# Second block: the values of all heads computed as [token, column] with the normed rows stationary

## The reference, cut to what matters

```python
h = rmsnorm(x, ln_attn_pre)
proj = h @ w_in                  # 1024 -> 3*512 (diff) + 3*512 (fox) + 8
dq, dk = first 512, next 512 columns     # 8 half heads of 64
dv = next 512 columns                    # 4 heads of 128
fq, fk, fv = the next 3 * 512 columns    # 8 heads of 64
f_logit = last 8 columns + b_f; cum = cumsum(log_sigmoid(f_logit))
# per block of 128 query rows, causal:
pd = softmax(dq dk^T / 8 + relative bias);  ad = pd[:, 0] - lam * pd[:, 1]
od = rmsnorm(ad @ dv, subln_g) * (1 - lambda_init)
pf = softmax(fq fk^T / 8 + cum_q - cum_k);  of = pf @ fv
x = x + rmsnorm(concat(od, of) @ w_out, ln_attn_post)
x = x + rmsnorm(square(relu(rmsnorm(x, ln_mlp_pre) @ w_up)) @ w_down, ln_mlp_post)
```

## Time and profile before

| | |
|---|---|
| time, median of 3 (range) | 1090.02 us (1089.85 to 1090.96) |
| the profiled execution | 1090.4 us, span 1089.1 us |
| TensorE busy | 1077.0 us, 99% of the span |
| TensorE weight loads | 885.4 us, 81% |
| ScalarE busy | 562.1 us, 52% |
| VectorE busy | 540.7 us, 50% |
| GpSimd busy | 434.8 us, 40% |
| mean granted TensorE clock | 0.998 |

### The profile page before, as it was taken

One profiled execution on the slowest core, in us unless ns is written; L12 is line 12 of the kernel. 1 busy time (PEld: TensorE's weight loads), 2 busy tenths in 40 slices (PEclk: granted clock), 3 DMA queues, 4 the chain that ended last, 5 costly groups with the idle time before them and its releaser, 6 DMA issues.

```text
span 1089.1 us, 14787 instructions
## 1 busy us (share of the span) xinstructions
PE 1077.0 (99%) x5656; PEld 885.4 (81%) x5656; DVE 540.7 (50%) x1136; ACT 562.1 (52%) x1042; POOL 434.8 (40%) x233
## 2 busy tenths in 40 slices
PE   8999999999999999999999999999999999999998
PEld 7877878787887888898778777789888888888886
DVE  3739799797765234152446455435111115544444
ACT  6546767767777642353556566554222224333333
POOL 4244242352532444552232332345444446444441
PEclk9999999999999999999999999999999999999999
DMA  9134131221312332722223221232333334323212
GB/s 255 52 92 122 40 79 49 69 78 39 97 50 68 90 92 92 249 78 62 79 78 84 72 79 58 85 90 79 97 97 97 97 97 135 99 97 98 95 57 78
DMA packets 140992, 98.02 MB, mean 90 GB/s; under 512 B 9077, under 2 KB 125170, under 8 KB 140922
## 3 DMA queue, kind: packets, MB, share of 16 engines
q1 hardware_dynamic: 139192, 95.83, 30.0%
q10 hardware_dynamic: 1730, 1.25, 0.4%
HBM read 94.93 MB, written 2.91 MB: 90 GB/s over the span
## 4 chain that ended last, share of the span: by engine, by line
PE 86%; DVE 9%; issue 2%; ACT 2%; DMA 1%; SPq 0%; POOL 0%; DVEq 0%; ACTq 0%
PE bank L496 26%; PE bank L1213 14%; PE bank L1231 14%; PE bank L537 5%; PE bank L910 4%; PE bank L884 4%; PE bank L894 4%; PE bank L1244 2%; DVE g L1915 1%; DVE bank L2033 1%; PE bank L511 1%; DVE multipliers L2031 1%; DVE s L2111 1%; PE bank L1059 1%; PE bank L1041 1%
## 5 line engine op out<-in xcount | busy, mean ns | idle before, releaser
L2497 POOL TENSOR_TENSOR ring<-raw_ring,ring 128x1024 fp32r<-128x1024 f32 x160 | 390.0, 2441 | 566.8 <-ACT ring L1258 566.7
L496 PE MATMUL bank<-hT,ring 128*128 128x512 f32 x1536 | 389.9, 401 | 0.5 <-ACT rawsb L1333 0.5
L496 PEld LDWEIGHTS bank<-hT,ring 128*128 128x128 f32 x1536 | 278.4, 188 | 57.1 <-issue 4.9
L1258 ACT CAST ring<-raw_ring 128x1024 fp32r<-128x1024 f32 x160 | 167.2, 1047 | 109.7 <-PE bank L1231 88.9
L1213 PE MATMUL bank<-hT,ring 128*128 128x512 f32 x672 | 152.5, 389 | 0.0
L1231 PE MATMUL bank<-ring,ring_u 128*128 128x512 f32 x672 | 152.5, 389 | 0.0
L1231 PEld LDWEIGHTS bank<-ring,ring_u 128*128 128x128 f32 x672 | 126.2, 188 | 26.2
L1213 PEld LDWEIGHTS bank<-hT,ring 128*128 128x128 f32 x672 | 126.1, 188 | 26.1
L2472 DVE TENSOR_TENSOR ring_u<-u,ring_u 128x1024 fp32r<-128x1024 f32 x32 | 80.7, 2529 | 73.8 <-ACT ring_u L1830 73.8
L2477 DVE TENSOR_TENSOR u<-u 128x512 f32<-128x512 f32 x32 | 22.9, 715 | 138.8 <-ACT u L1837 138.8
L1837 ACT ACTIVATE u<-bank 128x512 f32<-128x512 f32 x32 | 19.1, 598 | 114.9 <-PE bank L1213 108.4
(11 more groups left out here) (299 smaller groups left out, 1467.7 us busy)
## 6 DMA issues: line engine op xcount, KB each, us to landing
raw_ring<-in_w_in SPq DMA_DIRECT2D x144, 256.0 KB, 3.3
raw_ring<-in_w_up SPq DMA_DIRECT2D x64, 256.0 KB, 3.2
...
```

The lines of the kernel that those rows point to most:

```text
L496: p = pe.matmul(bank, m.slab_k8(n % 4)[:, a, k, :], m.hT[:, b, k, :], start=term == 0, stop=term == 23)
L1258: act.copy(m.ring[:, q, 0, :], m.raw_ring[:, q, :]).then_inc(s.slab_hi[q], 1)
L2497: pool.tensor_tensor(m.ring[:, q, 1, :], m.raw_ring[:, q, :], m.ring[:, q, 0, :].bitcast(F32), ALU.subtract).then_inc(s.slab_lo[q], 1)
```

## The change

The values no longer come as tiles. Eight products with 512 columns replace the eight value tiles: for each block j of 128 tokens, `hT` of these tokens is the stationary operand and a wide slab (256 rows by 512 value columns of w_in) the moving one, so that the result is [token, column] for four heads at once. Eight inner steps k run over four slabs, so each product needs all four slabs of a stage. The diff values are made first in the second block (`first_values`), in place of `next_halves`; the fox values inside head pair 0 (`ValuesAhead`). ScalarE copies each product into `v_rows`, from which `diff_av` and `fox_av` read. The tiles of q and k are four per head pair: those of head pair 0 ahead of it, those of head pair 1 in head pair 0 after the fox values, those of head pairs 2 and 3 in head pairs 1 and 2. Head pair 0 therefore holds 192 large matmuls, head pairs 1 and 2 hold 96 each; the places of the head's own products are scaled by 4/3 and 2/3 from the old ones out of 144 (`upto`). ScalarE's tile copies are moved to new places, the transposes of the values and their copies are gone, and GpSimd's `diff_rstd(i)` stands behind three splits of its head pair instead of four.

```diff
-B_COLS = [0, 512, 1024, 1536, 2048, 2560]
+B_COLS = [0, 512, 1536, 2048]
+B_RAW = [0, 1, 3, 4]
+VALUES, FORGET_VALUES = 0, 8
...
+def first_tile(i):
+    return 8 + 4 * i if i else 4
...
     for n in range(24):
-        i, c = divmod(n, 6)
-        tall(SLABS_B + n, w2, w2, B_COLS[c] + i * P, 4)
-        if n == 10:
+        if n // 4 in (VALUES // 4, FORGET_VALUES // 4):
+            wide(SLABS_B + n, w2, 2 * (n % 4), 1024 if n < 4 else 2560)
+        else:
+            i = 0 if n < 8 else n // 4 - 2
+            tall(SLABS_B + n, w2, w2, B_COLS[n % 4] + i * P, 4)
+        if n == 12:
             sp.wait_ge(s.small_dve, 29)
             sp.dma_start(m.cums, m.cumT).then_inc(s.cum_out, 16)
-        if n == 11:
+        if n == 13:
...
+    def value_products(bank, slab, j, ks, parts, first, last, ready=lambda k: None, release=False):
+        for k in ks:
+            n = slab + k // 2
+            pe.wait_ge(s.slab_lo[n % 4], n // 4 + 1)
+            ready(k)
+            for a, b in parts:
+                p = pe.matmul(bank, m.hT[:, b, k, j * P:(j + 1) * P], m.slab_k2(n % 4)[:, a, k % 2, :],
+                              start=first and k == 0 and (a, b) == parts[0], stop=last and k == KT - 1 and (a, b) == parts[-1])
+                yield p
+            if release and k % 2:
+                p.then_inc(s.slab_done[n % 4], 1)
+
+    def first_values(slab, scr):
...
+        for _ in value_products(bank[0], slab, 0, range(KT), PARTS, True, True, low(16)):
+            pass
+        for p in value_products(bank[1], slab, 1, range(KT), PARTS, True, True):
+            pass
+        p.then_inc(s.v_ps, 2)
+        norm_transposes(scr, 1, 1)
...
-    next_halves(SLABS_B, m.scr2, 1)
+    first_values(SLABS_B, m.scr2)
...
-        tiles = Tall(SLABS_B + 6 * (i + 1), 6, tile_b_free(6 * (i + 1)))
-        tiles.to(1)
-        diff_v_rows(i, pairs)
-        tiles.to(16)
-        fox_v_rows(i)
-        tiles.to(19)
+        tiles = Tall(SLABS_B + first_tile(i + 1), 4, tile_b_free(first_tile(i + 1))) if i else ValuesAhead()
+
+        def upto(place):
+            tiles.to(place * 2 // 3 if i else place * 4 // 3)
+
+        upto(19)
         diff_z_pair(i, 1, 0, pairs)
...
     for i in range(3):
-        g = 6 * (i + 1)
-        diff_v(i, 2)
         heads_high(i)
-        fox_v(i)
+        ahead(i, 0)
         fox_exp(i, 0, 0)
         fox_exp(i, 1, 0)
-        tile_b(g)
         diff_exp(i, 1, 0, 0)
...
         fox_p(i, 1, 0)
+        if i:
+            copies(i, 0)
+        ahead(i, 2)
...
         diff_exp(i, 0, 1, 1)
+        if i:
+            copies(i, 1)
+        ahead(i, 3)
         fox_p(i, 1, 2)
         fox_p(i, 0, 2)
-        tile_b(g + 3)
+        if i == 0:
+            copies(i, 0)
         fox_exp(i, 1, 3)
         fox_exp(i, 0, 3)
+        copies(i, 2 if i else 1)
         diff_p(i, 0, 1, 2)
         diff_p(i, 1, 1, 4)
         diff_square(i, 0, 1)
         diff_square(i, 1, 1)
         fox_p(i, 1, 3)
         fox_p(i, 0, 3)
-        tile_b(g + 4)
+        if i == 0:
+            copies(i, 2)
         fox_mix(i)
         diff_mix(i, 4)
-        tile_b(g + 5)
+        copies(i, 3)
...
     residual(0, SLABS_B)
-    for n in range(SLABS_B + 4, SLABS_B + 8):
+    for n in range(SLABS_B + 4, SLABS_B + 14):
         split(n)
     for i in range(3):
-        n = SLABS_B + 6 * i + 8
-        for q in range(4):
+        n = SLABS_B + 4 * i + 14
+        for q in range(3):
             split(n + q)
         diff_rstd(i)
-        split(n + 4)
-        split(n + 5)
+        split(n + 3)
```

191 lines of the change are left out of this document (116 added, 75 removed).

## The result

The changed kernel takes 1116.8 us (median of four, 1113.7 to 1118.4), against 1090.0 before: ratio 1.024, 95% interval 1.023 to 1.025. The profiled execution took 1115.3 us with a span of 1114.0, 24.9 more than before. The direction was as forecast, the size not: 1108 was predicted, with 1115 as the upper end, so the measured median lies above the stated range. TensorE's mean granted clock, 0.998 before, was 0.994 here and 0.989 to 0.994 in the four executions.

What follows compares the result with a forecast made beforehand. The prediction took TensorE, busy 99% of the span, as the bound. It summed 1090.4 - 2.8 - 0.3 + 2.5 + 2.5 + 10.8 + 5.2 = 1108.3 us, 1108 against the median, with a range of 1097 to 1115.

Steps and rivals of the forecast that it cites:

- next scores: End of head pairs 1 and 2: TensorE waits 0.7 us each for ScalarE's split of q and k.
- falls of the clock: TensorE's granted clock dropping to 0.50, its 1.2 GHz level, after waits; left out of the forecast's sum.
- rival 4: The clock falls after new TensorE waits, 1 to 1.7 us for each of three or four: 1112 to 1114; chance 0.13.
- The first stage: First value products: waits of 1.2 and 2.9 us for GpSimd's slab splits, 1.6 saved, so 2.5 us later.
- The first wait of head pair 0: At diff_mix, TensorE waits 2.4 to 2.5 us for VectorE's norm, since diff_rstd(0) stands behind a split.
- The waits in head pairs 1 and 2: With 48 of 144 cover matmuls lost, TensorE waits on the heads' chains: 5.4 us each, 10.8 for both.
- The lock: VectorE steps with two SBUF operands held up by GpSimd's splits: 2.6 us per head pair, 5.2 for both.
- rival 3: No lock between VectorE and GpSimd, chain waits alone: 1103 us; chance 0.2.
- The meeting with the first round: First split of head pairs 1 and 2 beside the last step of diff_weights(i, 0, 0): up to 2.2 us.
- The meeting with the second round's `diff_weights`: In head pairs 1 and 2, the next split meets this work and delays the last fox_max: up to 1.0 us.
- The saved work: TensorE work removed: value transposes, 2.8 and 0.3 us, and 1.6 us in the first stage of values.
- Rival 1: The cover is still enough, so only TensorE's savings of 3.8 + 1.6 count: 1085 us; chance 0.08.

Runs made afterwards that it cites:

- e4: Changed kernel with 11 unneeded matmuls put where TensorE waited 2.50 us for the fourth slab in the first value product: 1115.0 us.
- e7: Kernel with four edits together (1101.2 us), with diff_rstd of head pair 0 put back behind the third split: 1104.5 us.
- e11: Changed kernel with the first two value products taking the four slabs in turn, 12 matmuls on each: 1111.6 us.
- e1: Changed kernel with GpSimd splitting the fourth slab of the value stage ahead of two row norms: 1114.9 us.
- e2: Changed kernel with diff_rstd ahead of the third split in head pair 0 alone: 1114.7 us.
- e5: Changed kernel with the intermediate of diff_weights(i, 0, 0) kept in PSUM in head pairs 1 and 2: 1110.3 us.
- e8: Kernel with four edits together (1101.2 us), with tile matmul places rewritten in head pairs 1 and 2, and next q and k split earlier: 1108.2 us.
- e13: e10 with the casts of head pairs 1 and 2 back ahead of each tile's copy and diff_rstd ahead of the third split: 1104.8 us.
- e9: Kernel with four edits together (1101.2 us), with every second tile matmul of head pairs 1 and 2 issued twice: 1109.8 us.
- e10: e8's places with diff_mix at 89, the first stage of e11, the edits of e2 and e5, and casts moved in head pairs 1 and 2: 1088.35 us.
- e12: e10 with the places of the tile matmuls in head pairs 1 and 2 scaled by 2/3 again: 1091.2 us.

## Why the prediction was wrong

Against the profiled span of before, the prediction's terms and what they measured:

| | predicted | measured |
|---|---|---|
| ahead of the second block (478.27 to 477.71) | 0 | -0.6 |
| waits of before that are gone | 0 | -0.5 |
| less work on TensorE (the rest) | -4.7 | -1.7 |
| waits: first stage | 4.1 | 3.6 |
| waits: `diff_mix`, head pair 0 | 2.5 | 2.5 |
| waits of head pairs 1 and 2, lock and next scores with them | 16.0 | 14.8 |
| falls of the clock | 0 | 6.8 |
| sum | 17.9 | 24.9 |

(The row of head pairs 1 and 2 is 15.3 of the changed kernel, with the 1.3 at the first scores of head pair 3, less 0.5 that stood in the same lines before.)

**The step that failed** is rival 4: the falls of the clock were set aside as a case of their own, with a chance of 0.13, though the prediction itself counted up to six new waits of 2 to 3 us on TensorE. Their price, 1 to 1.7 each for three or four, was right: four of 1.70. It stood in the trace of before, in the neighbours of the window of the earlier trace rows:

```profile
8.00:10.00 2.00, 0.67 (x3) 0.67 (x4) 0.75 (x1) 1.17 (x2) 1.08 (x2) 0.79 1.15 345
...
12.00:14.00 2.00, 2.00 (x17) 2.00 (x15) 1.22 (x4) 2.00 (x5) 0.81 (x1) 0.86 1.20 298
```

With the 1.00 between them that fall lost 0.42 + 1.00 + 0.28 = 1.70, behind waits of 0.68 and 1.47. The argument against, clock 1.00 in 666 to 708 with 1.4 us idle, said nothing on waits of 2.5, since before had none there. Over all profiled executions of the changed kernel and its variants a fall followed 30 of 35 waits of 2.3 us or more, and 3 of 5 of 1.7 to 1.8. The five without are those at 613.86 and 634.31 above and the wait at `diff_mix` of head pair 0 in e4, e7 and e11. That part of the falls would only use up chain waits did not show either: the waits and the loss add up. The two things belonged in one sum: 1108 + 6.8 is 1115, and a range of 1097 to 1115 took in just one end of it.

**The first stage** was right in place and size. From the first product to the first tile after the stage it took 25.16 us before and 507.08 - 477.71 = 29.37 now, 4.2 more, which is the predicted 2.5 and one fall of 1.7 (both the waits and the work saved came out 0.5 smaller than derived, and these cancel). e1 and e11 show its cause: six matmuls use up a slab in 1.4 us and GpSimd needs 2.4.

**The first wait of head pair 0** was right (2.47 against 2.5), by e2.

**The waits in head pairs 1 and 2** were right in sum, 5.4 each without the lock: in head pair 1, 7.14 by the brackets, less the 1.7 that e5 took off. They were spread otherwise than derived, 2.3 at `diff_av(0, 1)` and little at `fox_z(3)`, and some 0.6 of the 2.3 is the lock again, as the next paragraph shows.

**The lock** exists: e5 shows it, and e8 and e13 have it in other steps; rival 3 falls. The meeting with the first round cost 3.0 us of waits over both head pairs (3.4 at L1077, less 0.5 that came up at L1125). The meeting with the second round's `diff_weights`, the 2.27 us step, took place as well, and delayed the last `fox_max` as derived:

```profile
629.20 0.28 PE L1106 MATMUL bank<-causal_b,ident_b 128*128 128x128 bf16 x2
...
630.15 0.68 DVE L2437 CUSTOM_DVE_ANT_0 b<-bank,cum 128x512 f32<-128x512 f32 x1
...
631.07 0.73 ACT L1785 ACTIVATE b<-b,stat 128x512 f32<-128x512 f32 x1 [2.86 <-DVE stat L2440]
```

In the round before, `fox_max` (L2437) started 0.32 us after L1106 did (621.36 to 621.04); here it started 0.95 after, right behind the late `diff_weights`. From the exponential at 631.07 on ScalarE had no gap until the `diff_p` for which TensorE waited at 634.31. So about 0.6 of that wait is the lock's, the same in head pair 2 (an estimate from these rows; no run took this meeting away alone). That makes some 4.2 us in all, against 5.2. It left the chain's own waits at nearer 4.8 than 5.4.

**The saved work** was put at 4.7, and 1.7 is found. Most of the rest is in head pairs 1 and 2. With full cover the heads' work is as derived (e9); with 96 matmuls e10's period is 38.06, less 0.41 of waiting 37.65, against 36.2, and the changed kernel's is 44.93, less 7.14 of waiting 37.8. So 1.4 to 1.6 us a head pair are neither listed as waits nor work that e9 has. A good part of it is waits too short for the list. In e10:

```profile
593.65 2.29 PE L506 MATMUL bank<-hT,ring 128*128 128x512 f32 x9
596.09 0.33 PE L1111 MATMUL bank<-consts,b 128*128 128x128 f32 x1
```

From the first of these nine to the next instruction it takes 2.44 us; in e9 twelve take 2.82 at the same place, so nine would take 2.14. A matmul's length is 0.39 and the spacing 0.228, so the first 0.16 us of a wait is hidden behind the end of the last matmul. This place and the next ones of the kind, ahead of 601.88, 611.78 and 613.02, add up to 0.9 of the 1.4; the remainder is open.

**Rival 1**, that the cover is still enough, was wrong for this order, but e10 shows it right for another: 1088.35 against its 1085. The prediction took the missing 48 matmuls for the cause; e9 seemed to confirm it, and e10, e12 and e13 show that what they had covered were, for the most part, late and locked splits.
